# A decoder layer with grouped experts: residual added where the expert outputs are written, and a last stage without TensorE

## The chip, the cores and the metric

The kernel runs on one core of a Trainium2 chip. The metric is the device time of one execution in microseconds (us). Times are medians over runs; the profile is of one execution, whose own time is given beside its span, the time from its first to its last instruction.

## What is computed

One step of a hybrid decoder layer, for 1024 prompt tokens and 64 sample tokens of width 1024, all in float32. The parts that matter here are the last two lines of the layer:

```
h = layer_norm(ALPHA * x + mix, ln1_g, ln1_b)
y = layer_norm(ALPHA * h + hier_moe(h, ...), ln2_g, ln2_b)
```

`hier_moe` sends each token to 2 of 32 experts (a group of 8 is picked first, then two in it). An expert computes `silu(h @ w_gate) * (h @ w_up) * gate`, 256 wide, and multiplies that by `w_down` back to 1024. A token's result is the sum of its two experts' rows. `layer_norm` takes mean and variance over the 1024 columns, scales by `1/sqrt(var + 1e-5)`, then multiplies by gamma and adds beta.

## The kernel before

The kernel works in stages that follow each other behind barriers: input projection and convolutions; gated delta rule, output projection and the first layer norm in tiles of 128 tokens (writing `h_dram`); routing, which fills a table of slots per expert; the experts; and a last stage with the second layer norm.

**The expert stage** (lines 1578 to 1849) runs 24 passes (`NPASS`) and then one more per full block of 128 slots that does not fit, here a single one. A pass handles 128 slots, 96 of an expert of its own and 32 of one expert that three passes share. Its steps, with their engines:

- POOL gathers the pass's rows of h from `h_dram` into `xg` by an indirect DMA (`gather`, L1650). There are two buffers, and a gather waits until TensorE has turned the rows that the buffer held (`xg_turned`).
- TensorE transposes them (`turn_x`, L1694), ACT and DVE copy half each out of PSUM (L1768, L1816), TensorE multiplies by the gate and up weights (`gate_up`), ACT and DVE form the activation (L1773, L1821), TensorE transposes it (`turn_ac`, L1700) and multiplies by the down weights (`down`).
- ACT and DVE copy half of the result each from PSUM to `yo` (`out_s` L1782, `out_v` L1826), and POOL scatters it to `picked_dram` by an indirect DMA (`scatter`, L1656). That array has two rows per token, one for each of its picks.

TensorE's order in pass q is written out by hand: `turn_x(q+1)`, `gate_up(q)`, `down(q-1)`, `turn_ac(q)`. POOL's is `gather(q+3)`, then `scatter(q-1)`. The weights (2 MB and 1 MB per pass, and as much again for each third pass's shared expert) come on SP's DMA queue into three buffers (`NA`), each load waiting for the pass that used the buffer. After the last of them SP loads all of h, nine tiles of 512 KB, into `hres` (L1622) for the last stage.

**The last stage** (L1851 to L2012) takes nine tiles of 128 tokens. SP loads a tile's two picks (`picked`, 1 MB). TensorE adds them with four products by the identity and so into PSUM (L1942). DVE forms `ALPHA * hres + ysum` (L1984), two `bn_stats` (L1988), `bn_aggr`, and two tiny operations on mean and variance (L1992, L1993). POOL raises the variance to the power -0.5 (L1914) and forms the shift (L1917). ACT normalises (L1951), DVE multiplies by gamma (L2000), POOL adds beta (L1922), and ACT issues the store (L1956). Three buffers rotate, and each engine works one tile behind the one before it: `both` does the front of tile t and then the gamma or beta step of tile t-1.

## Time and profile before

| What | Value |
|---|---|
| Median of 3 runs | 1169.77 us (1169.17 to 1171.09) |
| The profiled execution's own time | 1168.77 us |
| Its span | 1167.0 us, mean granted TensorE clock 0.915 |
| Busy over the span | PE 83%, DVE 34%, ACT 15%, POOL 19% |
| Experts, from the first gather to the last scatter's issue | 768.3 to 1103.5 us |
| Last stage, from the first load | 1108.5 to 1167.0 us |

The span's last 400 us are the experts and the last stage. The shares are means over stages with different limits, so each stage is read by itself.

### The profile page before, as it was taken

To read this page: it belongs to the slowest core of one execution; us is meant where nothing else is said; L and a number is where in the kernel's file an instruction comes from. 1 tells how busy PE (TensorE), PEld (TensorE's weight loads), DVE (VectorE), ACT (ScalarE), POOL (GpSimd) and SP (SyncE) were. 2 spreads that over 40 slices of the span, in tenths; PEclk is the share of its full clock that TensorE was granted. 3 is DMA by queue.
4 is the path that set the end of the run, shared out by engine and by line. 5 is a ranking of instruction groups with operands and counts; after the bars stand their busy time and mean duration, and the time that the engine had idled before them with its cause. 6 is when DMAs were issued, how large, how long until landed. Compare 5 with 4: busy or idle time off the path is not lost. (4 is left out here: it accounts for less than half of the span.)

```text
span 1167.0 us, 13262 instructions
## 1 busy us (share of the span) xinstructions
PE 971.8 (83%) x5403; PEld 547.1 (47%) x5403; DVE 393.2 (34%) x737; ACT 173.5 (15%) x357; POOL 226.7 (19%) x238
## 2 busy tenths in 40 slices
PE   6999999999887999999988762049999999995583
PEld 4666666655445666666765422023333333331231
DVE  0434332586005554545542344201111111110056
ACT  1222233111021111111100000011111111110012
POOL 1011111220013222221113100611121211201047
PEclk9999999999888999999998875569999999998787
DMA  6011110202425011110031007757999999996094
GB/s 259 19 37 37 37 37 32 61 34 56 142 76 184 10 46 37 45 45 31 24 112 51 28 1 279 276 161 291 378 422 418 414 411 387 395 391 235 0 332 163
DMA packets 61323, 186.51 MB, mean 160 GB/s; under 512 B 22984, under 2 KB 36328, under 8 KB 51720
## 3 DMA queue, kind: packets, MB, share of 16 engines
q1 hardware_dynamic: 34640, 157.73, 35.3%
q0 software_dynamic: 8208, 19.09, 4.4%
q10 hardware_dynamic: 18416, 8.86, 2.7%
q8 instruction: 43, 0.70, 0.2%
q14 instruction: 16, 0.13, 0.0%
HBM read 164.15 MB, written 30.01 MB: 166 GB/s over the span
## 5 line engine op out<-in xcount | busy, mean ns | idle before, releaser
L359 PE MATMUL pj<-xT,wblk 128*128 128x384 f32 (+1 forms) x960 | 300.0, 474 | 18.3 <-DMA xT<-in_xt_dram 9.2
L359 PEld LDWEIGHTS pj<-xT,wblk 128*128 128x128 f32 x960 | 183.3, 192 | 129.8 <-issue 17.7
L1708 PE MATMUL e<-wgu_s,xgT 128*32 128x512 f32 x384 | 170.9, 598 | 0.0
L1708 PE MATMUL e<-wgu_a,xgT 128*32 128x512 f32 x768 | 114.7, 600 | 6.2 <-issue 3.2
L1708 PE MATMUL e<-wdn_a,acT 128*32 128x512 f32 x576 | 86.8, 592 | 0.7 <-ACT acT L1777 0.7
L1708 PE MATMUL e<-szT,acT 128*32 128x512 f32 x192 | 86.3, 592 | 0.0
L1694 PE MATMUL e<-cst,xg 128*128 128x128 f32 x200 | 28.7, 291 | 65.2 <-DMA xg<-h_dram,lst 48.4
L994 PE MATMUL b<-wout,yaT 128*128 128x512 f32 x144 | 69.7, 630 | 3.8 <-DVE yaT L1319 3.8
L1821 DVE SCALAR_TENSOR_TENSOR ac<-sg,lst,e 128x256 f32<-128x256 f32 x24 | 11.5, 480 | 171.2 <-ACT sg L1773 171.2
L1656 POOL DMA_INDIRECT picked_dram<-yo,lst x24 | 24.1, 1005 | 229.3 <-PE e L1694 185.0
L1708 PEld LDWEIGHTS e<-wgu_a,xgT 128*32 128x32 f32 x768 | 32.3, 111 | 75.9 <-issue 72.4
L994 PE MATMUL b<-wout,ybt 128*128 128x512 f32 x144 | 65.1, 595 | 0.0
L1708 PE MATMUL e<-qkvT,xgT 128*32 128x512 f32 x384 | 56.5, 594 | 0.0
L1694 PEld LDWEIGHTS e<-cst,xg 128*128 128x128 f32 x200 | 24.6, 151 | 67.3 <-DMA xg<-h_dram,lst 50.5
L1708 PEld LDWEIGHTS e<-wdn_a,acT 128*32 128x32 f32 x576 | 24.7, 110 | 56.7 <-issue 55.7
L626 DVE SCALAR_TENSOR_TENSOR cv<-raw,small,cv 128x1112 f32<-128x1112 f32 x36 | 49.6, 1377 | 1.3
L1942 PE MATMUL ysum<-picked,cst 128*128 128x512 f32 x72 | 33.9, 634 | 12.5 <-DMA picked<-picked_dram 12.5
L624 DVE TENSOR_SCALAR cv<-raw,small 128x1112 f32<-128x1112 f32 x12 | 9.6, 800 | 102.8 <-ACT raw L473 102.7
L994 PEld LDWEIGHTS b<-wout,yaT 128*128 128x128 f32 x144 | 27.7, 202 | 33.4 <-issue 28.8
L1708 PEld LDWEIGHTS e<-wgu_s,xgT 128*32 128x32 f32 x384 | 40.5, 110 | 0.0
L1826 DVE COPY yo<-e 128x512 f32<-128x512 f32 x25 | 17.3, 692 | 68.1 <-PE e L1708 63.3
L1816 DVE COPY xgT<-e 128x512 f32<-128x512 f32 x25 | 17.3, 691 | 66.0 <-PE e L1694 66.0
(321 smaller groups left out, 1248.4 us busy)
## 6 DMA issues: line engine op xcount, KB each, us to landing
wgu_a<-in_w_gate_up_dram SPq DMA_DIRECT2D x17, 2048.0 KB, 22.4
wdn_a<-in_w_down_dram SPq DMA_DIRECT2D x25, 1024.0 KB, 13.9
wgu_s<-in_w_gate_up_dram SPq DMA_DIRECT2D x8, 2048.0 KB, 15.6
qkvT<-in_w_gate_up_dram SPq DMA_DIRECT2D x8, 2048.0 KB, 19.4
wblk<-in_wcol_dram SPq DMA_DIRECT2D x20, 512.0 KB, 3.3
szT<-in_w_down_dram SPq DMA_DIRECT2D x8, 1024.0 KB, 18.1
picked<-picked_dram SPq DMA_DIRECT2D x8, 1024.0 KB, 5.7
h_dram<-h SPq DMA_DIRECT2D x9, 512.0 KB, 2.6
```

Of the source, the lines that this page charges most:

```text
L359: last = pe.matmul(pj[par][:, bank * 512:bank * 512 + m], wblk[par][:, k, :], xT[:, k, a:a + m], start=(k == 0), stop=(k == KT - 1))
L624: ins = dve.tensor_scalar(out, raw[par][:, 0:CFLAT], w, None, ALU.mult)
L626: ins = dve.scalar_tensor_tensor(out=out, in0=raw[par][:, j:CFLAT + j], scalar=w, in1=out, op0=ALU.mult, op1=ALU.add)
L994: last = pe.matmul(b[6 + half][:, :], src[:, kk, :], wout[:, k, half * 512:(half + 1) * 512], start=(k == H), stop=(k == H - 1))
L1656: pool.indirect_dma_start(y2_d, bass.IndirectOffsetOnAxis(ap=lst[:, q, 0:1], axis=0), yo[q % 2][:, :], None, bounds_check=2 * TP - 1, oob_ ...
L1694: last = pe.transpose(bank[:, at:at + P], xg[k][:, c * P:(c + 1) * P], C("ident"))
L1708: last = pe.matmul(out[at, :], lhsT[:, at], theirs if j == GROUP - 1 else mine, start=start, stop=stop)
L1816: dve.tensor_copy(xgT[k][:, H:, :].rearrange("p c t -> p (c t)"), b[1][:, :]).then_inc(xgT_ready, 1)
L1821: dve.scalar_tensor_tensor(out=ac[k][:, :], in0=sg[k][:, :], scalar=entry.bitcast(F32), in1=b[2 + k][:, FE:], op0=ALU.mult, op1=ALU.mult). ...
L1826: dve.tensor_copy(yo[k][:, 512:], b[7][:, :]).then_inc(yo_ready, 1)
L1942: last = pe.matmul(ysum[k][:, half * 512:(half + 1) * 512], C("ident"), picked[k][:, at:at + 512], start=(pick == 0), stop=(pick == 1))
```

## The change

- Each slot's table entry had the token number in its fourth word; it now has ALPHA for the first pick and 0 for the second.
- `out_v` does both halves on DVE: yo = (fourth word) x (gathered row) + (product in PSUM). ACT's `out_s` is gone. The sum of a token's two picks thus holds ALPHA * h.
- The gathered row must stay until then. `xg` has four buffers (`NX`), two of them in the space of `hres`, and `gather(q)` waits for `yo_ready` of pass q-4 where it waited for `xg_turned` of pass q-2. POOL issues four gathers first, and then in turn `scatter(q-1)`, `gather(q+3)`.
- The nine loads of `hres` are gone.
- The last stage has no TensorE work. DVE adds the two picks (`tensor_tensor`, both inputs in SBUF), takes the statistics, and after ACT's square root does a reciprocal and the shift. ACT normalises into a new tile `fin`. Gamma is split: DVE takes columns 0 to 511 (of the tile before), POOL columns 512 to 1023, then POOL adds beta to the whole. SP issues the stores, ACT the loads of gamma and beta. Four buffers rotate, and the loops are written out.

```
         rows_of = qkvT[:, :, :].rearrange("p c t -> p (c t)")
-        hres = rows_of[:, 0:NT * D].rearrange("p (t d) -> p t d", d=D)
...
                     for k in range(2):
-                        dve.tensor_copy(entry[:, k, :, 3], C("token"))
+                        dve.memset(entry[:, k, :, 3].bitcast(F32), ALPHA if k == 0 else 0.0)
                         dve.tensor_copy(entry[:, k, :, 1], C("token"))
...
-            xg, xgT = two("xg", [P, D]), two("xgT", [P, KT, P])
+            NX = 4
+            xg = [sb(f"xg{k}", [P, D], ctx=c4)[:, :] for k in range(2)] + [rows_of[:, k * D:(k + 1) * D] for k in range(2)]
+            xgT = two("xgT", [P, KT, P])
...
                         if q % (GROUP - 1) == GROUP - 2 and g < NE // GROUP:
                             load_shared_gu(g)
                             load_shared_dn(g)
-                    for t in range(NT):
-                        sp.dma_start(hres[:, t, :], h_d[t * P:(t + 1) * P, :]).then_inc(hres_in, 16)
-
...
-                    for k in pr:
-                        pool.memset(xg[k][:, :], 0.0).then_inc(cleared, 1)
-                    e.wait_ge(cleared, 2)
+                    for k in range(NX):
+                        pool.memset(xg[k], 0.0).then_inc(cleared, 1)
+                    e.wait_ge(cleared, NX)
...
                     def gather(q):
                         if q % (GROUP - 1) == 0:
                             e.wait_ge(lst_in[q // (GROUP - 1)], 32)
-                        wait(e, xg_turned, q - 1)
-                        pool.indirect_dma_start(xg[q % 2][:, :], None, h_d,
+                        wait(e, yo_ready, 2 * (q - NX + 1))
+                        pool.indirect_dma_start(xg[q % NX], None, h_d,
...
                     def scatter(q):
                         e.wait_ge(yo_ready, 2 * q + 2)
                         pool.indirect_dma_start(y2_d, bass.IndirectOffsetOnAxis(ap=lst[:, q, 0:1], axis=0),
                                                 yo[q % 2][:, :], None, bounds_check=2 * TP - 1, oob_is_err=False
                                                 ).then_inc(ov_scattered if q == last else scattered[q % 2], 16)
-                    for q in range(3):
+                    for q in range(NX):
                         gather(q)
-                    for q in range(NPASS):
-                        if q + 3 < NPASS:
-                            gather(q + 3)
-                        if q >= 1:
-                            scatter(q - 1)
+                    for q in range(1, NPASS):
+                        scatter(q - 1)
+                        if q + NX - 1 < NPASS:
+                            gather(q + NX - 1)
...
                     def turn_x(i, k):
                         wait(e, xgT_ready, 2 * i)
+                        rows = xg[k]
                         for c in range(KT):
                             bank, at = b[c // H], (c % H) * P
-                            last = pe.transpose(bank[:, at:at + P], xg[k][:, c * P:(c + 1) * P], C("ident"))
+                            last = pe.transpose(bank[:, at:at + P], rows[:, c * P:(c + 1) * P], C("ident"))
                         last.then_inc(xg_turned, 1)
...
                         if q + 1 < NPASS:
-                            e.wait_ge(gathered[(q + 1) % 2], 16 * ((q + 1) // 2) + 16)
-                            turn_x(q + 1, (q + 1) % 2)
+                            e.wait_ge(gathered[(q + 1) % NX], 16 * ((q + 1) // NX) + 16)
+                            turn_x(q + 1, (q + 1) % NX)
...
-                def out_s(e, i, k):
-                    e.wait_ge(dn_done, i + 1)
-                    act.activation(yo[k][:, 0:512], b[6][:, :], ACT.Copy).then_inc(yo_ready, 1)
...
                         silu(e, q, q % 2)
-                        if q >= 1:
-                            wait(e, scattered[(q - 1) % 2], 16 * ((q - 1) // 2))
-                            out_s(e, q - 1, (q - 1) % 2)
                         ac_turned_s(e, q, q % 2)
...
-                def out_v(e, i, k):
+                def out_v(e, i, k, rows, entry):
                     e.wait_ge(dn_done, i + 1)
-                    dve.tensor_copy(yo[k][:, 512:], b[7][:, :]).then_inc(yo_ready, 1)
+                    for half in range(2):
+                        c = slice(half * 512, (half + 1) * 512)
+                        dve.scalar_tensor_tensor(out=yo[k][:, c], in0=rows[:, c], scalar=entry.bitcast(F32),
+                                                 in1=b[6 + half][:, :], op0=ALU.mult, op1=ALU.add).then_inc(yo_ready, 1)
...
-            NB = 3
+            NB = 4
...
-            picked, res = each("picked", [P, 2 * D]), each("res", [P, D])
+            picked, res, fin = each("picked", [P, 2 * D]), each("res", [P, D]), each("fin", [P, D])
...
-            ysum = [pb(f"ysum{k}", [P, D], c5) for k in pr]
...
             with nc.Block() as block:
                 @block.sync
                 def _(e):
                     y2_v = y2_d.rearrange("(t k) d -> t (k d)", k=2)
...
+                    for t in range(NT):
+                        wait(e, summed, t - NB + 1)
+                        m = rows_in(t)
+                        sp.dma_start(picked[t % NB][0:m, :], y2_v[t * P:t * P + m, :]).then_inc(in_ready[t % NB], 16)
+                    for t in range(NT):
+                        m = rows_in(t)
+                        e.wait_ge(out_ready, t + 1)
+                        out = ys_o.rearrange("s t d -> (s t) d") if t == PT else yp_o[0, t * P:(t + 1) * P, :]
+                        sp.dma_start(out, fin[t % NB][0:m, :]).then_inc(stored[t % NB], 16)
...
+                @block.scalar
+                def _(e):
+                    act.dma_start(lng[:, :], ln2g_d.broadcast_to((P, D))).then_inc(ln_in, 16)
+                    act.dma_start(lnb[:, :], ln2b_d.broadcast_to((P, D))).then_inc(ln_in, 16)
+                    e.wait_ge(eps_ready, 1)
+                    for t in range(NT):
+                        k = t % NB
+                        e.wait_ge(var_ready, t + 1)
+                        act.activation(dev[k][:, :], mv[k][:, 1:2], ACT.Sqrt, bias=eps[:, :]).then_inc(dev_ready, 1)
+                        e.wait_ge(shift_ready, t + 1)
+                        wait(e, stored[k], 16 * (t // NB))
+                        act.activation(fin[k][:, :], res[k][:, :], ACT.Identity, scale=rstd[k][:, :],
+                                       bias=shift[k][:, :]).then_inc(normed, 1)
 
                 @block.gpsimd
                 def _(e):
+                    pool.memset(eps[:, :], LN_EPS).then_inc(eps_ready, 1)
                     e.wait_ge(ln_in, 32)
...
-                        pool.tensor_tensor(rstd[k][:, :], mv[k][:, 1:2], mhalf[:, 0:1], ALU.pow).then_inc(rstd1[k], 1)
...
-                        pool.tensor_tensor(shift[k][:, :], mv[k][:, 0:1], rstd[k][:, :], ALU.mult
-                                           ).then_inc(rstd_ready[k], 1)
...
-                        e.wait_ge(g_ready[k], i + 1)
-                        pool.tensor_tensor(done(i, k), done(i, k), lnb[:, :], ALU.add).then_inc(out_ready[k], 1)
...
+                    for t in range(NT):
+                        k = t % NB
+                        e.wait_ge(normed, t + 1)
+                        pool.tensor_tensor(fin[k][:, hi], fin[k][:, hi], lng[:, hi], ALU.mult).then_inc(scaled_p, 1)
+                        e.wait_ge(scaled_p, t + 1)
+                        e.wait_ge(scaled_v, t + 1)
+                        pool.tensor_tensor(fin[k][:, :], fin[k][:, :], lnb[:, :], ALU.add).then_inc(out_ready, 1)
 
                 @block.vector
                 def _(e):
...
-                        dve.scalar_tensor_tensor(out=r, in0=done(i, k), scalar=ALPHA, in1=ysum[k][:, :],
-                                                 op0=ALU.mult, op1=ALU.add).then_inc(ysum_read[k], 1)
...
+                    def front(t):
+
+                        k, m = t % NB, rows_in(t)
+                        e.wait_ge(in_ready[k], 16 * (t // NB) + 16)
+                        wait(e, normed, t - NB + 1)
+                        dve.tensor_tensor(res[k][0:m, :], picked[k][0:m, 0:D], picked[k][0:m, D:], ALU.add
+                                          ).then_inc(summed, 1)
+                        e.wait_ge(summed, t + 1)
+                        for half, c in enumerate((lo, hi)):
+                            last = dve.bn_stats(stats[k][:, half, :], res[k][:, c])
                         link(last)
...
-                        link(dve.bn_aggr(mv[k][:, :], stats[k][:, :, :].rearrange("p a b -> p (a b)")))
-                        dve.tensor_scalar(mv[k][:, 0:1], mv[k][:, 0:1], -1.0, None, ALU.mult)
-                        dve.tensor_scalar(mv[k][:, 1:2], mv[k][:, 1:2], LN_EPS, None, ALU.add
-                                          ).then_inc(var_ready[k], 1)
...
+                        dve.bn_aggr(mv[k][:, :], stats[k][:, :, :].rearrange("p a b -> p (a b)")).then_inc(var_ready, 1)
+
+                    def scale(t):
+
+                        k = t % NB
+                        if t == 0:
...
-                        dve.tensor_tensor(done(i, k), done(i, k), lng[:, :], ALU.mult).then_inc(g_ready[k], 1)
+                        e.wait_ge(normed, t + 1)
+                        dve.tensor_tensor(fin[k][:, lo], fin[k][:, lo], lng[:, lo], ALU.mult).then_inc(scaled_v, 1)
+
+                    def finish(t):
+
+                        k = t % NB
+                        e.wait_ge(dev_ready, t + 1)
+                        link(dve.reciprocal(rstd[k][:, :], dev[k][:, :]))
+                        dve.scalar_tensor_tensor(out=shift[k][:, :], in0=mv[k][:, 0:1], scalar=-1.0, in1=rstd[k][:, :],
+                                                 op0=ALU.mult, op1=ALU.mult).then_inc(shift_ready, 1)
+                    for t in range(NT):
+                        front(t)
+                        if t >= 1:
+                            scale(t - 1)
+                        finish(t)
+                    scale(NT - 1)
```

On POOL's queue, at the start of the expert stage, before (`picked_dram<-yo` is a scatter, `xg<-h_dram` a gather):

```order
L1639 MEMSET xg 128x1024 x2
L1650 DMA xg<-h_dram,lst 128x1024 x5
L1656 DMA picked_dram<-yo,lst 2304x1024
L1650 DMA xg<-h_dram,lst 128x1024
L1656 DMA picked_dram<-yo,lst 2304x1024
L1650 DMA xg<-h_dram,lst 128x1024
```

and now (the two buffers in the old `hres` space go by the name `qkvT`):

```order
L1636 MEMSET xg 128x1024 x2
L1636 MEMSET qkvT 128x1024 x2
L1647 DMA xg<-h_dram,lst 128x1024 x2
L1647 DMA qkvT<-h_dram,lst 128x1024 x2
L1653 DMA picked_dram<-yo,lst 2304x1024
L1647 DMA xg<-h_dram,lst 128x1024
L1653 DMA picked_dram<-yo,lst 2304x1024
```

Five gathers stood ahead of the first scatter, and now four: from there on a gather is issued behind the same scatter as before, but for the pass before the one it served.

On DVE's queue, one tile in the last stage's loop, before:

```order
L1984 SCALAR_TENSOR_TENSOR res<-qkvT,ysum 128x1024
L1988 BN_STATS stats<-res 128x6 x2
L1990 MEMSET spare 128x1
L1991 BN_AGGR mv<-stats 128x2
L1992 TENSOR_SCALAR mv<-mv 128x1
L1993 TENSOR_SCALAR mv<-mv 128x1
L2000 TENSOR_TENSOR qkvT<-qkvT,ln2g 128x1024
```

and now:

```order
L1922 TENSOR_TENSOR res<-picked 128x1024
L1926 BN_STATS stats<-res 128x6 x2
L1928 MEMSET spare 128x1
L1929 BN_AGGR mv<-stats 128x2
L1937 TENSOR_TENSOR fin<-fin,ln2g 128x512
L1943 RECIPROCAL rstd<-dev 128x1
L1944 SCALAR_TENSOR_TENSOR shift<-mv,rstd 128x1
```

The first operation now has both inputs in SBUF, the gamma step is half as wide, and the reciprocal and the shift stand behind it, before the next tile's sum.

## Rows read from the trace of the kernel before

**Rows 1.** Windows: us, PE, PEld, DVE, ACT, POOL busy, PE clock, DMA share, GB/s

```profile
845.00:892.00 47.00, 46.84 (x432) 16.99 (x424) 7.46 (x12) 7.41 (x16) 8.07 (x8) 1.00 1.01 421
```

**Rows 2.** Timeline, PE's idle gaps in passes: start, us, instruction, [idle before]

```profile
918.79 0.63 PE L1708 MATMUL e<-wgu_a,xgT 128*32 128x512 f32 x3 [1.67 <-DVE xgT L1816]
...
956.39 0.63 PE L1708 MATMUL e<-wgu_a,xgT 128*32 128x512 f32 x3 [2.49 <-issue]
...
992.89 0.63 PE L1708 MATMUL e<-wgu_a,xgT 128*32 128x512 f32 x3 [1.39 <-DVE xgT L1816]
```

**Rows 3.** Timeline, two pass boundaries: PE's transposes of gathered rows

```profile
799.05 1.04 PE L1694 MATMUL e<-cst,xg 128*128 128x128 f32 x8
...
810.73 1.04 PE L1694 MATMUL e<-cst,xg 128*128 128x128 f32 x8
```

**Rows 4.** Timeline, the first of these boundaries: DVE's copy, POOL's scatter and gather

```profile
798.91 0.69 DVE L1826 COPY yo<-e 128x512 f32<-128x512 f32 x1 [2.54 <-PE e L1708]
...
800.40 1.00 POOL L1656 DMA_INDIRECT picked_dram<-yo,lst  x1 [10.23 <-PE e L1694]
801.71 1.01 POOL L1650 DMA_INDIRECT xg<-h_dram,lst  x1 [0.30 <-issue]
```

**Rows 5.** DMA issues: gathers of 801.71, 825.14, all 19 after 801.6; median us to landing

```profile
xg<-h_dram,lst POOLq DMA_INDIRECT x1, 9.8
...
xg<-h_dram,lst POOLq DMA_INDIRECT x1, 14.3
...
xg<-h_dram,lst POOLq DMA_INDIRECT x19, 13.3
```

**Rows 6.** Groups by line and form, DVE: busy us, mean ns

```profile
L1210 DVE SCALAR_TENSOR_TENSOR xt<-xt,b 128x512 f32<-128x512 f32 x18 | 11.6, 683 | 28.0 <-PE b L994 28.0
```

**Rows 7.** Timeline, SP's queue: the loads of `hres`

```profile
1039.43 7.81 SPq L1622 DMA_DIRECT2D qkvT<-h_dram  x9
```

**Rows 8.** Timeline, last stage: the first loads and the last store

```profile
1108.47 0.81 SPq L1882 DMA_DIRECT2D picked<-picked_dram  x2
...
1162.41 0.61 ACTq L1967 DMA_DIRECT2D out_dram<-qkvT  x1
```

**Rows 9.** DMA issues of the first two loads there: count, KB each, median us to landing

```profile
picked<-picked_dram SPq DMA_DIRECT2D x2, 1024.0 KB, 6.0
```

**Rows 10.** Timeline, one tile of the last stage, DVE, POOL and ACT

```profile
1128.39 1.29 DVE L1988 BATCH_NORM_STATS2 stats<-res 128x6 f32<-128x512 f32 x2
1129.72 0.20 DVE L1991 BATCH_NORM_AGGREGATE mv<-stats 128x2 f32<-128x12 f32 x1
...
1130.09 1.22 DVE L2000 TENSOR_TENSOR qkvT<-qkvT,ln2g 128x1024 f32<-128x1024 f32 x1
...
1130.26 1.46 POOL L1914 TENSOR_TENSOR rstd<-mv,mhalf 128x1 f32<-128x1 f32 x1
...
1131.94 2.37 POOL L1922 TENSOR_TENSOR qkvT<-qkvT,ln2b 128x1024 f32<-128x1024 f32 x1
1132.02 1.24 ACT L1951 ACTIVATE qkvT<-res,shift,rstd 128x1024 f32<-128x1024 f32 x1 [2.84 <-POOL shift L1917]
```

**Rows 11.** Timeline, an earlier stage: DVE with two SBUF inputs beside POOL

```profile
352.60 2.37 POOL L959 TENSOR_TENSOR kq<-qkvT,egr 128x1024 f32<-128x1024 f32 x1
352.72 2.82 DVE L1332 TENSOR_TENSOR dT<-dT,rn2b 128x512 f32<-128x512 f32 x1 [0.85 <-POOL dT L955]
```

**Rows 12.** Groups by form: mean ns of such steps, the power in an earlier stage

```profile
L1332 DVE TENSOR_TENSOR dT<-dT,rn2b 128x512 f32<-128x512 f32 x7 | 4.8, 684 | 0.0
...
L946 POOL TENSOR_TENSOR rstd<-mv,mhalf 128x1 f32<-128x1 f32 x9 | 5.0, 550 | 167.1 <-DVE mv L1225 167.1
...
L955 POOL TENSOR_TENSOR dT<-dT,cst 128x512 f32<-128x512 f32 x9 | 11.4, 1271 | 8.1 <-ACT dT L1160 8.1
```

**Rows 13.** Groups: ACT's table load and a small ACT step

```profile
L1773 ACT ACT_TABLE_LOAD x1 | 1.3, 1283 | 0.0
L1464 ACT ACTIVATE gb<-ga 128x36 f32<-128x36 f32 x1 | 0.2, 232 | 10.3 <-DVE ga L1492 10.3
```

More of the change, by code:

```diff
@@ L1864, in build, with rows_in @@
             stats, mv = each("stats2", [P, 2, 6]), each("mv2", [P, 2])
[L1865 removed]
+            dev, rstd, shift = each("dev2", [P, 1]), each("rstd2", [P, 1]), each("shift2", [P, 1])
+            eps = sb("eps2", [P, 1], ctx=c5)
             spare = sb("spare5", [P, 1], ctx=c5)
[L1867 removed]
             S = phase(c5)
[L1869 to L1873 removed]
+            ln_in, chn, eps_ready = S("ln2_in"), S("chn2"), S("eps_ready")
+            in_ready, stored = ([S(f"{n}{k}") for k in pr] for n in ("in_ready", "stored"))
+            summed, var_ready, dev_ready, shift_ready, normed, scaled_v, scaled_p, out_ready = (S(n) for n in (
+                "summed", "var_ready", "dev_ready", "shift_ready", "normed", "scaled_v", "scaled_p", "out_ready"))
+            lo, hi = slice(0, D // 2), slice(D // 2, D)
+            def rows_in(t):
+                return NS if t == PT else P
             with nc.Block() as block:
@@ L1888, in _ @@
-                    load(0, 2)
-                    with e.Fori(1, NT // NB - 1) as i:
-                        for k in pr:
-                            load(i, k)
-                    for k in pr:
-                        load(NT // NB - 1, k, P if k < NB - 1 else NS)
-                    for k in pr:
-                        e.wait_ge(stored[k], 16 * (NT // NB))
-                def done(i, k):
-                    return hres[:, ds(NB * i + k, 1), :].rearrange("p a d -> p (a d)")
-                def rounds(e, step):
-                    def body(i):
-                        for k in pr:
-                            step(i, k)
-                    turns(e, NT // NB, body)
+                    for t in range(NT):
+                        wait(e, summed, t - NB + 1)
+                        m = rows_in(t)
+                        sp.dma_start(picked[t % NB][0:m, :], y2_v[t * P:t * P + m, :]).then_inc(in_ready[t % NB], 16)
@@ L1920, in add_bias @@
-                    def add_bias(i, k):
-                        e.wait_ge(g_ready[k], i + 1)
-                        pool.tensor_tensor(done(i, k), done(i, k), lnb[:, :], ALU.add).then_inc(out_ready[k], 1)
-                    def both(i, k):
-                        step(i, k)
-                        if k > 0:
-                            add_bias(i, k - 1)
-                        elif not isinstance(i, int):
-                            add_bias(i - 1, NB - 1)
-                    rounds(e, both)
@@ L1931, in _ @@
-                    add_bias(NT // NB - 1, NB - 1)
-                @block.tensor
-                def _(e):
-                    def step(i, k):
-                        e.wait_ge(in_ready[k], 16 * i + 16)
-                        wait(e, ysum_read[k], i)
-                        for half in range(2):
-                            for pick in range(2):
-                                at = pick * D + half * 512
-                                last = pe.matmul(ysum[k][:, half * 512:(half + 1) * 512], C("ident"),
-                                                 picked[k][:, at:at + 512], start=(pick == 0), stop=(pick == 1))
-                        last.then_inc(summed[k], 1)
-                    rounds(e, step)
@@ L1947, in _ @@
-                @block.scalar
-                def _(e):
-                    def step(i, k):
-                        e.wait_ge(rstd_ready[k], i + 1)
-                        act.activation(done(i, k), res[k][:, :], ACT.Identity, scale=rstd[k][:, :],
-                                       bias=shift[k][:, :]).then_inc(norm_ready[k], 1)
-                    def store(i, k):
-                        e.wait_ge(out_ready[k], i + 1)
-                        act.dma_start(yp_o[0, ds((NB * i + k) * P, P), :], done(i, k)).then_inc(stored[k], 16)
-                    def both(i, k):
-                        step(i, k)
-                        if k > 0:
-                            store(i, k - 1)
-                        elif not isinstance(i, int):
-                            store(i - 1, NB - 1)
-                    rounds(e, both)
-                    e.wait_ge(out_ready[NB - 1], NT // NB)
-                    act.dma_start(ys_o.rearrange("s t d -> (s t) d"), hres[0:NS, NT - 1, :]
-                                  ).then_inc(stored[NB - 1], 16)
+                    for t in range(NT):
[5 more added lines that the diff above has]
+                        pool.tensor_tensor(fin[k][:, :], fin[k][:, :], lnb[:, :], ALU.add).then_inc(out_ready, 1)
@@ L1970, in _ @@
                 @block.vector
                 def _(e):
-                    def front(i, k):
-                        at = (NB * i + k) * 2
-                        ln = [0]
-                        def link(ins):
-                            ln[0] += 1
-                            ins.then_inc(chn, 1)
-                            e.wait_ge(chn, at + ln[0])
-                        e.wait_ge(summed[k], i + 1)
-                        wait(e, norm_ready[k], i)
-                        r = res[k][:, :]
-                        dve.scalar_tensor_tensor(out=r, in0=done(i, k), scalar=ALPHA, in1=ysum[k][:, :],
-                                                 op0=ALU.mult, op1=ALU.add).then_inc(ysum_read[k], 1)
-                        e.wait_ge(ysum_read[k], i + 1)
-                        for half in range(2):
-                            last = dve.bn_stats(stats[k][:, half, :], r[:, half * 512:(half + 1) * 512])
+                    chain = [0]
```

52 lines of the change are left out of this document (12 added, 40 removed).

## The prediction

> **What bounds the kernel now.** I read the windows first, to see which resource is full in the expert stage, then the waits of TensorE there, then the timeline of one pass boundary and of one tile in the last stage. Over 47 us in the middle of the expert stage TensorE is busy for 46.84 us at the full clock (1.00, its 2.4 GHz level), and at the same time the DMA engines' share is 1.01 [rows 1]. Two limits lie on top of each other: a pass is 11.68 us of TensorE work (799.05 to 810.73 [rows 3]), and its transfers take about as long. TensorE's only sizeable gaps are three, of 1.67, 2.49 and 1.39 us, each before a `gate_up` [rows 2], whose inputs are the expert weights: 5.5 us in all. So the stage has no slack for a transfer that arrives later. In the last stage POOL is the bound: power, shift and beta follow each other without a gap from 1130.26 to 1134.31 [rows 10], about 4.1 us a tile, and the power takes 1.46 us there against 0.55 elsewhere [rows 10, 12].
>
> **The expert stage: the gather is issued later.** Before, the gather behind `scatter(0)` was the sixth, number 5, needed by `turn_x(5)` at the start of pass 4. Now it is number 4, needed at the start of pass 3. In the time of before: DVE's copy starts at 798.91 and takes 0.69, the scatter follows at 800.40 and the gather at 801.71 [rows 4]. Now DVE does both halves as multiply-adds from PSUM, and such steps take 0.683 us [rows 6], starting about 0.61 apart, so `yo` is ready 0.6 later and the gather starts at 802.3. The transposes that need it start at 810.73 [rows 3]: it has 8.4 us. Number 5 had 20.7 us before, from 801.71 to 810.73 + 11.68. Landings took 9.8 us at 801.71, 14.3 at 825.14, and 13.3 in the median of the 19 from 801.6 on [rows 5]. It is late.
>
> What a late gather costs is less than its lateness, for a stall S in one pass lengthens that pass and gives the next gather more time: S(n+1) = L - 8.4 - S(n), with L the landing time. So the mean stall is (L - 8.4)/2. Twenty gathers (4 to 23) are issued this way. L is unknown, for the stalls also thin the traffic. The bounds are from the rows: at 9.8 (the lightest such row) 0.7 us each, 14 us in all; at 13.3 (the full queue) 2.45 each, 49 us. A cycle of three passes has one with the shared expert's 3 MB on top. The rows nearest to a queue that starts nearly empty are 9.8, 9.8 and 14.3, mean 11.3; I take the middle between that and 13.3, L = 12.3, as the stalls let the queue drain only in part: 20 x 3.9/2 = 39 us. The 5.5 us of waits for weights [rows 2] are then gone, since TensorE asks for weights later. **Net +33.5 us**, ends +8.5 and +43.5.
>
> The rule of the Trainium skill on queues (DMA: Bandwidth & Descriptors, Queues, rings and completion order) says that a DMA engine takes turns between queue rows, a packet from each; read as equal halves, that would let a gather land before its deadline even beside the weights. The trace does not bear that reading out, with 13.3 us for half a megabyte at most; the case of a gather in time is the second rival.
>
> Other edits there. ACT's copies go, and DVE's second one is on no path in the passes: `down(q)` needs the bank only after a `gate_up`. In the single extra pass, and in the scatter that it waits for, it is: 0.6 us twice, **+1.2 us**. The loads of `hres` cost nothing now (issued from 1039.43 for 7.81 us [rows 7], when the last weights were requested, and awaited by nobody before the last stage), so their removal gives nothing. Two more clears of `xg` on POOL stand ahead of the first gather, where POOL has to wait for the lists of slots anyway.
>
> **The last stage.** From the first load's issue to the last store's it takes 1162.41 - 1108.47 = 53.94 us [rows 8]. What decides it now is whether DVE and POOL can read SBUF at the same time. They can't, if DVE has two inputs there [rows 11]: L1332 usually takes 0.684 us [rows 12] and took 2.82 beside a POOL operation that ended at 354.97, that is, it ran after it. In the other direction POOL's one-element power takes 1.46 instead of 0.55 us when DVE's gamma product (two inputs in SBUF) began just before [rows 10, 12]. Before, only that product was of this kind. Now the sum, the gamma half and the shift are, beside POOL's gamma half and beta.
>
> One period, from the end of a DVE gamma half: POOL starts beta after 0.06 and holds the port for 2.35; DVE's reciprocal (0.2, as the aggregate) fits beside it, its shift must wait and ends at 2.6; the next sum takes 1.2 (as L2000 [rows 10]), to 3.8; the statistics 1.29, to 5.1, while ACT normalises and POOL does its gamma half (1.27, L955 [rows 12]); the aggregate with its links 0.26; DVE's gamma half 0.68: **6.0 us** per tile against 4.1. Whether a one-element DVE step waits too no row shows; if not, the period is 5.84 (the sum then waits), and the stage 2.7 us less. I take 6.0, after POOL's one-element step.
>
> The Trainium skill (SBUF — State Buffer, Who interferes with whom) calls the port pair an exclusive lock and names DVE steps with two SBUF inputs beside a POOL read, of any size. By it the shift waits as well, and the period would be 6.0.
>
> The sum in steps: first load 6.0 [rows 9], with gamma and beta now beside it; sum, statistics and aggregate 2.75; table load 1.28 and square root 0.23 [rows 13]; reciprocal, shift and links 0.5; seven periods 42.1 (tile 1 to tile 8); sum, statistics, aggregate of tile 8 2.75; then gamma half of tile 7 0.7, beta of tile 7 2.4, shift 0.2, normalise 1.3, DVE's half 0.7, POOL's half 1.3, beta 2.35: 9.0. Together 64.6 us, **+10.7**. The table load is on the path once (it stands behind the wait for the first variance). The same skill (ScalarE: Activation LUTs, What ACT_TABLE_LOAD costs) adds 1.38 us of drain to it, which no row here shows; the sum would be 12.1. TensorE's 72 products go, and save only the head, some 5 us, which is in this sum. SP's stores stand behind its last load; buffer 0 is stored just in time for tile 4.
>
> **Sum.** 33.5 + 1.2 + 10.7 = +45.4 us on the profiled execution, 1168.77 + 45.4 = 1214.2. The median lies 1.0 above that execution, so 1215.
>
> **Rivals.**
> - *The gathers are late, but the port is shared without exclusion* (10%). Against it stand [rows 11]. Then POOL is the bound with 1.27 + 2.35 us a tile, 3.7 with links, and the last stage takes 47.6 us, -6.3: 1169.8 + 33.5 + 1.2 - 6.3 = 1198.
> - *The gathers land in time* (6%). For it: a gather alone on thin traffic is small, and 9.8 is close to 8.4. Against it: no row after 801.6 is below 9.8. The stage then gains or loses nothing, or gains up to 5.5 if the weights also come earlier: 1169.8 + 1.2 + 10.7 = 1182, down to 1176.
> - *It gets faster, by the last stage* (3%): no exclusion, so the head that TensorE took is a gain and the stage is 6.3 us shorter. It decides the sign only where the expert stage costs less than 5 us net, 10 x (L - 8.4) - 5.5, that is for L below 9.4. With L = 8.4: 1169.8 + 1.2 - 6.3 = 1165.
> - *The change does less than it says*: if something else had long set the pass (weights), the later gather would hide behind it (1%, 1180). TensorE's 46.84 us in 47 [rows 1] speak against it.
> - The likeliest case has 80%.
>
> **How the numbers follow.** 1215 is the likeliest. Its own ends are 1169.8 + 8.5 + 1.2 + 8.0 = 1187 and 1169.8 + 43.5 + 1.2 + 13 = 1228, the 13 with a first load that is slowed by gamma and beta. The range of 8 in 10 takes in most of this and the first rival, 1186 to 1229. Runs of this kernel differ by 0.16%, so 0.2% is what a measurement can tell from no change. Faster takes the third rival, 0.03; same 0.02, where ends of the second and the third meet; slower 0.95.
>
> **What would show it.** In the changed profile: TensorE idle before the transposes of `xg`, released by the gathers, 1 to 6 us in most passes and some 35 to 40 in all, while the DMA share falls under 1.00; gaps before `gate_up` gone. In the last stage a period of 6.0 us, the shift on DVE lasting some 2 us though it has one element, and POOL waiting in turn. Wrong would be: gathers that land in under 8.4 us; a period of 3.7 to 4.1; or a granted clock under 1.00 in the passes, which the gaps could bring (it is 1.00 now [rows 1]) and which is not in the sum.

## The result, and the profile after

| | before | after |
|---|---|---|
| Median of 4 runs each | 1169.47 us (1166.23 to 1171.09) | 1219.95 us (1218.48 to 1222.14) |
| Ratio | | 1.0446, interval 1.0416 to 1.0475 |
| Profiled execution: own time, span, granted clock | 1168.77, 1167.0, 0.915 | 1218.81, 1217.0, 0.887 |

The kernel is 4.5% slower; the forecast was 1215 us. The profiled execution's span grew by 50.0 us. Cut at the same events in both traces:

| Stretch | Forecast | Measured |
|---|---|---|
| to the first `turn_x` (772.6, now 773.33) | 0 | +0.7 |
| first to last `turn_x` (266.6, now 308.24): waits for gathers | +39 | +32.3 |
| the same: waits for weights gone | -5.5 | -5.5 |
| the same: the rest, nearly all TensorE at its lower clock | not in the sum | +14.8 |
| last `turn_x` to the last stage's first load (69.25, now 70.1) | +1.2 | +0.9 |
| first load to last store (53.94, now 61.0) | +10.7 | +7.1 |
| behind the last store | 0 | -0.3 |

What TensorE waited for from 800 to 1085 us, in the profile's waits after (us in total, times, longest):

```profile
PE e L1691 <- DMA xg<-h_dram,lst: 18.1, 7, 5.8
PE e L1691 <- DMA qkvT<-h_dram,lst: 14.2, 7, 5.4
```

Both are `turn_x` waiting for its gathered rows (`qkvT` names the two buffers in the old space of `hres`). No wait for weights is left, where there were three [rows 2]. The boundary of pass 0 on POOL, in the timeline after (start, duration):

```profile
801.50 0.99 POOL L1653 DMA_INDIRECT picked_dram<-yo,lst  x1 [27.41 <-DVE yo L1813]
802.80 1.02 POOL L1647 DMA_INDIRECT xg<-h_dram,lst  x1 [0.30 <-issue]
813.18 1.00 POOL L1653 DMA_INDIRECT picked_dram<-yo,lst  x1 [9.37 <-DVE yo L1813]
814.48 1.00 POOL L1647 DMA_INDIRECT xg<-h_dram,lst  x1 [0.30 <-issue]
```

The first late gather starts at 802.80; 802.3 was forecast from [rows 4]. The 20 gathers from there on take 8.8 to 14.3 us to land, mean 11.66. TensorE behind some of its waits, in the timeline after:

```profile
811.75 1.09 PE L1691 MATMUL e<-cst,xg 128*128 128x128 f32 x8 [0.47 <-DMA xg<-h_dram,lst]
...
841.23 1.97 PE L1691 MATMUL e<-cst,qkvT 128*128 128x128 f32 x8 [5.41 <-DMA qkvT<-h_dram,lst]
843.13 1.08 PE L1705 MATMUL e<-qkvT,xgT 128*32 128x512 f32 x3
843.15 1.06 PE L1705 MATMUL e<-wgu_s,xgT 128*32 128x512 f32 x1
...
868.72 1.41 PE L1691 MATMUL e<-cst,xg 128*128 128x128 f32 x8 [1.90 <-DMA xg<-h_dram,lst]
...
884.09 1.10 PE L1691 MATMUL e<-cst,xg 128*128 128x128 f32 x8 [1.84 <-DMA xg<-h_dram,lst]
...
969.00 1.97 PE L1691 MATMUL e<-cst,qkvT 128*128 128x128 f32 x8 [4.15 <-DMA qkvT<-h_dram,lst]
```

Behind waits of 0.47 and 1.84 us the eight transposes take 1.1 us. Behind those of 4 us and more they take 1.97, and the first products then 1.08, where they take 0.6 otherwise. Behind the wait of 1.90 us the transposes are slowed half-way (1.41). The windows after show the reason in their granted clock (columns: window, its length, busy us and count of PE, PEld, DVE, ACT and POOL, granted clock, DMA share, GB/s); the last row is the window of [rows 1]:

```profile
834.80:838.00 3.20, 1.03 (x10) 0.20 (x2) 1.41 (x2) 0.38 (x1) 0.20 (x1) 1.00 1.04 434
838.00:841.20 3.20, 0.00 (x0) 0.00 (x0) 0.00 (x0) 0.00 (x0) 1.81 (x2) 0.60 1.02 435
841.20:843.00 1.80, 1.77 (x8) 1.57 (x8) 0.00 (x0) 0.00 (x0) 0.00 (x0) 0.50 0.96 394
843.00:845.00 2.00, 2.00 (x13) 0.56 (x16) 0.69 (x1) 0.60 (x1) 0.00 (x0) 0.50 1.02 428
845.00:847.00 2.00, 2.00 (x24) 0.53 (x20) 0.00 (x0) 0.00 (x0) 0.00 (x0) 0.89 1.08 455
...
845.00:892.00 47.00, 43.26 (x378) 14.00 (x374) 7.64 (x12) 4.10 (x9) 6.05 (x6) 0.96 0.90 361
```

The clock falls to 0.50 (1.2 GHz) while TensorE is idle, stays there for some 4 us of work, and is back at 1.00 (2.4 GHz) by 847. So this pass takes 13.74 us from 841.23, and not 11.68 [rows 3]. Six passes are long in this way: those from 841.23, 868.72, 926.34, 969.00, 998.03 and 1054.41, by 2.1, 1.9, 2.2, 3.0, 1.9 and 3.0 us without the waits at their ends, some 14 of the 14.8. In the two long by 3.0 us the clock stays low for 6 us of work. Four of them follow waits of 4.15 to 5.79 us, two (868.72, 998.03) waits of 1.90 and 2.48.

The last stage, one tile on DVE and POOL, in the timeline after:

```profile
1171.39 0.64 DVE L1937 TENSOR_TENSOR fin<-fin,ln2g 128x512 f32<-128x512 f32 x1
1171.94 0.15 DVE L1943 RECIPROCAL rstd<-dev 128x1 f32<-128x1 f32 x1
1172.13 0.16 DVE L1944 SCALAR_TENSOR_TENSOR shift<-mv,rstd 128x1 f32<-128x1 f32 x1
1172.21 3.39 DVE L1922 TENSOR_TENSOR res<-picked 128x1024 f32<-128x1024 f32 x1
1175.63 1.29 DVE L1926 BATCH_NORM_STATS2 stats<-res 128x6 f32<-128x512 f32 x2
1176.96 0.20 DVE L1929 BATCH_NORM_AGGREGATE mv<-stats 128x2 f32<-128x12 f32 x1
1177.08 0.64 DVE L1937 TENSOR_TENSOR fin<-fin,ln2g 128x512 f32<-128x512 f32 x1
```

```profile
1172.17 2.34 POOL L1906 TENSOR_TENSOR fin<-fin,ln2b 128x1024 f32<-128x1024 f32 x1 [1.14 <-DVE fin L1937]
1174.48 2.24 POOL L1903 TENSOR_TENSOR fin<-fin,ln2g 128x512 f32<-128x512 f32 x1
```

DVE's sum, 1.2 us of work (each is 1.22 in e7 below), is recorded with 3.39 us: POOL's beta started 0.04 us before it, ends at 1174.51, and the sum ends 1.1 us later. It waited for beta; e6 and e7 below test this. POOL's gamma half then waits for the sum (2.24 us where alone it takes 1.26). The period (from one tile to the next) is 5.70 us, against 4.1 before [rows 10]. It changes once, at ACT's fifth normalisation (ACT, SP and DVE after):

```profile
1188.04 1.24 ACT L1893 ACTIVATE fin<-res,shift,rstd 128x1024 f32<-128x1024 f32 x1 [4.85 <-DMA out_dram<-fin]
```

```profile
1151.70 30.10 SPq L1873 DMA_DIRECT2D picked<-picked_dram  x9
1181.84 31.40 SPq L1878 DMA_DIRECT2D out_dram<-fin  x9
```

```profile
1190.11 1.03 DVE L1944 SCALAR_TENSOR_TENSOR shift<-mv,rstd 128x1 f32<-128x1 f32 x1
1191.06 1.21 DVE L1922 TENSOR_TENSOR res<-picked 128x1024 f32<-128x1024 f32 x1
```

Buffer 0 isn't stored in time, since SP issues its first store at 1181.84, behind all nine loads. After that wait the two engines meet in another order: now the one-element shift is the step that waits, the sum takes 1.21 us, POOL's beta waits for it (3.28), and the period is 5.02 us.

### The profile page after: what moved, and what is told of

The parts are those of the page before. It is cut to its first block and busy times, and to the rows that moved or that the text cites. A ratio compares the mean times of both kernels' runs of the same rounds, so it can differ in the third digit from the quotient of the medians.

```text
span 1217.0 us, 13017 instructions
## 1 busy us (share of the span) xinstructions
PE 952.6 (78%) x5331; PEld 532.5 (44%) x5331; DVE 419.7 (34%) x762; ACT 165.1 (14%) x342; POOL 234.1 (19%) x232
## 5 line engine op out<-in xcount | busy, mean ns | idle before, releaser
L1705 PE MATMUL e<-wgu_s,xgT 128*32 128x512 f32 x384 | 180.0, 624 | 0.0
L1705 PE MATMUL e<-wgu_a,xgT 128*32 128x512 f32 x768 | 117.3, 612 | 0.0
L1691 PE MATMUL e<-cst,xg 128*128 128x128 f32 x104 | 18.7, 339 | 85.0 <-DMA xg<-h_dram,lst 67.2
L1705 PE MATMUL e<-qkvT,xgT 128*32 128x512 f32 x384 | 63.1, 649 | 0.0
L1691 PEld LDWEIGHTS e<-cst,xg 128*128 128x128 f32 x104 | 15.0, 174 | 88.8 <-DMA xg<-h_dram,lst 69.7
L994 PEld LDWEIGHTS b<-wout,ybt 128*128 128x128 f32 x144 | 26.0, 190 | 26.2 <-issue 26.2
L946 POOL TENSOR_TENSOR rstd<-mv,mhalf 128x1 f32<-128x1 f32 x9 | 5.0, 552 | 167.0 <-DVE mv L1225 167.0
```

Source lines behind the costliest of these rows:

```text
L994: last = pe.matmul(b[6 + half][:, :], src[:, kk, :], wout[:, k, half * 512:(half + 1) * 512], start=(k == H), stop=(k == H - 1))
L1691: last = pe.transpose(bank[:, at:at + P], rows[:, c * P:(c + 1) * P], C("ident"))
L1705: last = pe.matmul(out[at, :], lhsT[:, at], theirs if j == GROUP - 1 else mine, start=start, stop=stop)
```

## The experiments

**e1: a fifth row buffer.** If the late gathers are what the expert stage lost by, letting each start one pass earlier must give it all back, clock included.

```
-            NX = 4
+            NX = 5
...
-            xg = [...] + [rows_of[:, k * D:(k + 1) * D] for k in range(2)]
+            xg = [...] + [rows_of[:, k * D:(k + 1) * D] for k in range(3)]
```

> The changed kernel with five buffers for gathered rows (NX = 5), so that a gather is again issued two passes ahead. Theory (late gathers): the 32 us of waits for gathers and the 14 us that the passes lose at the lower clock both go, the waits for weights (5.5 us) come back; what is left against the kernel before is the last stage (+7), the extra pass (+1) and the clears (+1): 1178 to 1180 us. Rival (the lateness is not the cause; DVE's doubled copy or the holding of rows until the outputs are written is): still above 1210 us.

1180.22 us (1177.97 to 1181.22), at the upper end of the forecast; ratio to before 1.0083 [1.0057, 1.0108]. (The ratios of the experiments are to runs of the kernel before that were made beside them, medians 1169.66 us for e1 to e4 and 1170.18 for e5 to e8.) TensorE's waits in e1 from 798 us on and a window of the passes (columns as above):

```profile
PE e L1705 <- issue: 3.4, 1, 3.4
PE e L1705 <- DVE xgT L1801: 1.5, 1, 1.5
PE e L1705 <- DVE yo L1813: 1.3, 1, 1.3
...
PE e L1705 <- ACT xgT L1765: 0.9, 1, 0.9
```

```profile
845.00:892.00 47.00, 47.00 (x432) 16.43 (x428) 9.95 (x16) 5.46 (x12) 8.06 (x8) 1.00 1.01 421
```

No gather is waited for in the passes, the waits before `gate_up` are back, and in this window clock and DMA share stand at 1.00 and 1.01 as in [rows 1]. (Behind the one wait of 3.4 us the clock was at 0.50 for some 2.6 us of work.) From first to last `turn_x` it takes 267.1 us (before 266.6). So the whole of the +41.6 us came from when the gathers start; the multiply-adds on DVE and the residual in the table cost the passes 0.5 us at most. Of the 11.6 us by which e1's profiled span is still above that of before, 6.8 are the last stage and 3.6 stand ahead of the first `turn_x`. Of these, 3.2 are there already when POOL starts its first clear, ahead of anything that the edit touches.

**e2: the kernel before, with the gathers late.** Only POOL's order is changed, to that of the change; two buffers, `hres` and the old last stage stay.

```
-                    for q in range(3):
+                    for q in range(4):
                         gather(q)
-                    for q in range(NPASS):
+                    for q in range(1, NPASS):
+                        scatter(q - 1)
                         if q + 3 < NPASS:
                             gather(q + 3)
-                        if q >= 1:
-                            scatter(q - 1)
```

> The kernel before with POOL's order alone changed to that of the changed kernel (four gathers, then scatter(q-1) ahead of gather(q+3)); residual, loads of h and last stage as before. Theory (late gathers): the gather has 9.0 us (801.71 to 810.73), so waits of (11.7 - 9.0)/2 in 20 passes are 27 us, and falls of the clock add up to 14, less the 5.5 for weights: 1195 to 1206 us. Rival (the residual in the expert stage or the missing loads of h cost the time): 1169 to 1172 us.

1206.46 us (1200.06 to 1210.76), half a microsecond over the forecast; ratio 1.0293 [1.0256, 1.0330]. Its runs spread over 10.7 us, those of e1 over 3.3, so its middle is less sure. Its waits and one window:

```profile
PE e L1693 <- DMA xg<-h_dram,lst: 29.5, 14, 5.0
```

```profile
900.00:947.00 47.00, 42.00 (x360) 14.07 (x362) 6.29 (x10) 6.16 (x13) 6.05 (x6) 0.91 0.80 319
```

Fourteen waits as in the change, and a fallen clock. In the profiled execution, the slowest of the four, first to last `turn_x` is 306.2 us, +39.6: of it 29.5 waits, -5.5 weights, and again a rest of 15.6. The order alone makes the loss; what the change does on DVE and ACT isn't needed for it.

**e3: the change, with TensorE kept busy in the gaps.** Is the rest of 14.8 us the clock? Six products that nobody reads (into bank 0, once its last contents are copied) stand ahead of the waits for four of the gathers that came late.

```
+                        if q + 1 in (6, 12, 15, 21):
+                            wait(e, xgT_ready, 2 * (q + 1))
+                            for _ in range(6):
+                                pe.matmul(b[0][:, :], C("ident"), cst[:, 0:512], start=True, stop=True)
                         if q + 1 < NPASS:
                             e.wait_ge(gathered[(q + 1) % NX], 16 * ((q + 1) // NX) + 16)
```

> The changed kernel with six 128x512 products without use put on TensorE in front of the waits for gathers 6, 12, 15 and 21, the four behind which it waited over 4 us and the granted clock then fell; they write a PSUM bank that the transposes overwrite. Theory (the fallen clock lengthens those passes by 2.1, 2.2, 3.0 and 3.0 us): the clock stays at 1.00 in these stretches and the time falls by 5 to 10 us, to 1210 to 1215 us, though TensorE has more to do. Rival (these passes are long because of their transfers, the clock is a by-product): 1219 to 1222 us or more.

1214.39 us (1211.76 to 1215.73), ratio 1.0383 [1.0359, 1.0407], 5.6 us under the change though TensorE has more to do. What stands in its timeline where the change had the gap before 841.23 (the profile lists the six products as 12 records), and two windows where the change had such gaps:

```profile
836.73 5.32 PE L1737 MATMUL e<-cst 128*128 128x512 f32 x12
842.41 1.09 PE L1691 MATMUL e<-cst,qkvT 128*128 128x128 f32 x8 [0.37 <-DMA qkvT<-h_dram,lst]
```

```profile
834.00:852.00 18.00, 17.63 (x126) 6.37 (x122) 2.63 (x5) 1.36 (x3) 2.01 (x2) 1.00 1.01 426
918.00:936.00 18.00, 18.00 (x134) 6.54 (x130) 2.77 (x5) 1.36 (x3) 2.02 (x2) 1.00 1.00 419
```

The transposes start even later than in the change (842.41 for 841.23), and take 1.09 us and not 1.97. First to last `turn_x` is 299.6 us. Waits of 13.2 and four times 5.32 us of empty products make 34.5 us, 2.2 more than the change's 32.3 of waiting; with -5.5 for the weights a rest of 4 is left of the 14.8. So the lower clock in these four places made some 10 us of the rest. Net it cost less, 8.6 us from first to last `turn_x`, as the waits grew by those 2.2: a pass that isn't slowed leaves the next gather less time. The 4 that are left hold two new falls of the clock, behind waits of 3.21 and 4.38 us.

**e5 to e7: what sets the last stage.** All three start from e1. e5 issues the stores among the loads; e6 gives DVE the whole of gamma, so that POOL has only beta; e7 leaves POOL's work out, so the second half of its columns lacks gamma and all of them lack beta.

```
 e5 (SP), behind the load of tile t:
+                        if t >= NB + 1:
+                            store(t - NB - 1)
 e6 (POOL, DVE):
-                        pool.tensor_tensor(fin[k][:, hi], fin[k][:, hi], lng[:, hi], ALU.mult).then_inc(scaled_p, 1)
-                        e.wait_ge(scaled_p, t + 1)
...
-                        dve.tensor_tensor(fin[k][:, lo], fin[k][:, lo], lng[:, lo], ALU.mult).then_inc(scaled_v, 1)
+                        dve.tensor_tensor(fin[k][:, :], fin[k][:, :], lng[:, :], ALU.mult).then_inc(scaled_v, 1)
 e7 (POOL), in place of the gamma half and beta:
+                        pool.memset(eps2[:, t:t + 1], 0.0).then_inc(out_ready, 1)
```

> The kernel of the first experiment (the change with five row buffers, 1180.2 us) with one edit in the last stage: SP issues the store of tile t-5 behind the load of tile t, so that no store stands behind all nine loads. It removes one wait of ScalarE's final activation for a store, 4.5 us there. Theory of the port (vectorE and GpSimd hold each other off the tiles in SBUF, and the tile pace of 5.70 us comes from that): the wait was mostly slack, and the pace of 5.70 us now runs on to the end where it was 5.0 us after the wait, so the two about cancel: 1178 to 1182 us. Rival, the wait counted whole: 1175.7 us.

> The five-buffer kernel (1180.2 us) with gamma multiplied by vectorE on all 1024 columns (1.24 us in place of 0.64) and no gamma half on GpSimd, whose only work per tile is then the bias, 2.34 us. Where the two engines exclude each other, the tiles' period is gamma 1.2 + bias 2.3 + sum 1.2 + statistics 1.3 + 0.2 and about 0.2 of gaps, since the bias starts when gamma ends and holds the next sum off: 6.0 to 6.4 us, so 1182 to 1187 us, although GpSimd has less to do. Rival, no exclusion (the long sums of 3.4 us have another cause, such as the loads): vectorE's own work, 4.5 us a tile, sets the pace: about 1170 us.

> The five-buffer kernel (1180.2 us) with GpSimd's gamma half and bias left out of the last stage (the second half of the columns isn't scaled and no column gets its bias; one element is set instead, so that the order of the work stays). Exclusion: no sum takes 3.4 us any more, every one takes 1.2, the tile pace is vectorE's own 3.8 to 3.9 us instead of 5.7 to 5.0, and the end of the last tile is some 5 us shorter too: 1160 to 1166 us. Rival, the sums are slow because of the loads that land beside them: they keep 3.4 us, the pace stays at 5.7, and only the last tile's 4.6 us go: 1175.6 us.

| | Median, us | Ratio to before | Period in the trace |
|---|---|---|---|
| e1 | 1180.22 | 1.0083 [1.0057, 1.0108] | 5.70, then 5.0 |
| e5 | 1180.26 (1175.41 to 1182.22) | 1.0083 [1.0054, 1.0113] | 5.69 to the end |
| e6 | 1181.73 (1177.33 to 1184.06) | 1.0099 [1.0071, 1.0126] | 6.23 |
| e7 | 1163.46 (1158.61 to 1166.99) | 0.9948 [0.9929, 0.9967] | 3.53, but for one wait for a store |

Two tiles' sums on DVE in each, first e5, then e6 with its gamma and POOL's beta, then e7:

```profile
1134.02 3.38 DVE L1927 TENSOR_TENSOR res<-picked 128x1024 f32<-128x1024 f32 x1
...
1139.72 3.38 DVE L1927 TENSOR_TENSOR res<-picked 128x1024 f32<-128x1024 f32 x1
```

```profile
1139.19 1.17 DVE L1935 TENSOR_TENSOR fin<-fin,ln2g 128x1024 f32<-128x1024 f32 x1
...
1140.50 2.35 POOL L1904 TENSOR_TENSOR fin<-fin,ln2b 128x1024 f32<-128x1024 f32 x1 [3.88 <-DVE fin L1935]
...
1140.55 3.39 DVE L1920 TENSOR_TENSOR res<-picked 128x1024 f32<-128x1024 f32 x1
```

```profile
1126.78 1.22 DVE L1921 TENSOR_TENSOR res<-picked 128x1024 f32<-128x1024 f32 x1
...
1130.30 1.22 DVE L1921 TENSOR_TENSOR res<-picked 128x1024 f32<-128x1024 f32 x1
```

e6 is the sharpest: POOL has a third less to do and is idle for 3.88 us a tile, and still the period grows to 6.23 us, inside the 6.0 to 6.4 worked out for two engines that hold each other off. The rival, DVE's own work setting the pace, put the period at 4.5 us and the time at 1170 (e7's 3.53 and the wider gamma would make an estimated 4.1). The median is 0.3 us under the forecast and its interval overlaps e1's, so that e6 is slower than e1 rests on the period. e7 shows the other side: without POOL's operations no sum is long, at the same loads, and the period is DVE's own. The clash with POOL costs 2.2 us a tile at the pace of 5.70, and 1.5 at that of 5.02. e5 removes the wait for the store and gains nothing, because the pace of 5.69 us then goes on to the end: the wait was paid for by the better order behind it.

**e4, e8: a last stage without the clash.** The gathers early as in e1; TensorE sums the picks into PSUM as in the kernel before (without the multiply-add of `hres`, which the sum now holds); DVE reads PSUM for the statistics and for (sum - mean) x gamma; ACT scales by 1/deviation; POOL adds beta alone. e8 also issues the stores as e5 does.

```
+                                last = pe.matmul(ysum[k][:, half * 512:(half + 1) * 512], C("ident"),
+                                                 picked[k][:, at:at + 512], start=(pick == 0), stop=(pick == 1))
...
+                            last = dve.bn_stats(stats[k][:, half, :], ysum[k][:, c])
...
+                        dve.scalar_tensor_tensor(out=res[k][:, :], in0=ysum[k][:, :], scalar=mv[k][:, 0:1],
+                                                 in1=lng[:, :], op0=ALU.subtract, op1=ALU.mult).then_inc(scaled_v, 1)
...
+                        act.activation(fin[k][:, :], res[k][:, :], ACT.Copy, scale=rstd[k][:, :]).then_inc(normed, 1)
```

> Five buffers, and another last stage: TensorE adds the picks into PSUM as in the kernel before, the statistics read PSUM, DVE forms (sum - mean) * gamma in one step from PSUM and SBUF, ACT multiplies by 1/deviation, POOL adds beta alone. No DVE step has two inputs in SBUF, so by the theory of the exclusive port nothing holds POOL or DVE: the period is TensorE's 3.8 us, the stage some 50 us instead of 61, and the time 1166 to 1169 us. Rival (DVE and POOL slow each other whatever their inputs are): beta takes over 2.4 us or the DVE step over 1.3 us, and the time is 1172 us or more.

> The fourth experiment's kernel (1164.5 us) with the stores issued among the loads as in the fifth. ScalarE's wait of 6.5 us for a store goes. Its trace has a pace of 3.43 us a tile before the wait and 2.83 after it, and the last activation started at 1155.6 us; at 3.43 all the way it would start at 1126.9 + 8 x 3.43 = 1154.3. So 1162.5 to 1164.5 us, 1.3 below. Rival, the wait counted whole: 1158 us.

e4: 1164.52 us (1161.41 to 1167.44), ratio 0.9960 [0.9939, 0.9980]. e8: 1165.15 us (1160.91 to 1167.41), ratio 0.9961 [0.9943, 0.9978]. Both are better than the change, and 0.4% better than the kernel before, with intervals that leave out 1. DVE in e8:

```profile
1134.09 1.28 DVE L1948 SCALAR_TENSOR_TENSOR res<-ysum,mv,ln2g 128x1024 f32<-128x1024 f32 x1
1135.29 0.15 DVE L1951 RECIPROCAL rstd<-dev 128x1 f32<-128x1 f32 x1
1135.95 1.30 DVE L1937 BATCH_NORM_STATS2 stats<-ysum 128x6 f32<-128x512 f32 x2 [0.50 <-PE ysum L1897]
```

and POOL in e8:

```profile
1133.28 2.35 POOL L1922 TENSOR_TENSOR fin<-fin,ln2b 128x1024 f32<-128x1024 f32 x1 [0.53 <-ACT fin L1913]
```

The two run side by side at their own durations, the multiply at 1.28 us with one input in PSUM. DVE waits 0.50 us a tile for TensorE's sum, which makes the period of 3.43 us. With the other edits of this last stage made at the same time, the runs don't say what each is worth by itself; e4's forecast, 1166 to 1169 us, was too high, in part because it took 3.8 us for TensorE's period.

e4 has a wait of 6.5 us for the store and catches most of it up afterwards. The last activation on ACT, in e4 and in e8:

```profile
1155.60 1.15 ACT L1908 ACTIVATE fin<-res,rstd 128x1024 f32<-128x1024 f32 x1 [1.09 <-DVE rstd L1946]
```

```profile
1156.51 1.15 ACT L1913 ACTIVATE fin<-res,rstd 128x1024 f32<-128x1024 f32 x1 [1.09 <-DVE rstd L1951]
```

The last stage's first load stands at 1110.19 in e4 and at 1112.41 in e8. From there to this activation it is 45.4 us in e4 and 44.1 in e8: the forecast gain of 1.3 us is there in the traces. The medians don't show it (e8's lies 0.6 above e4's, within both spreads, and over the forecast), as the stages ahead of the last differ by more than that from run to run.

## Where the prediction held, and where not

- *The late gathers are the main loss*: held, and shown by e1 and e2. The first late gather had from 802.80 to 811.28, where `turn_x` began to wait: 8.5 us for the forecast 8.4. The formula 20 x (L - 8.4)/2 gives 32.6 us with the measured L of 11.66, against 32.3 of waits. That they agree so closely is partly luck: six of the 20 gathers had landed in time, where the formula lets a stall go under nought, and a pass at the lower clock hid part of the next wait, which it leaves out. The choice "L = 12.3" was too high: the nearest rows' mean, 11.3, would have been better than the middle between that and the full queue. In the four windows of 47 us from 845 to 1033 the DMA share was 0.81 to 0.94, before 0.96 to 1.01.
- *The clock*: this is the step that failed. "a granted clock under 1.00 in the passes, which the gaps could bring [...] and which is not in the sum" is a term put at nothing. It cost 14.8 us, near a third of the whole loss, and e3 took some 10 of them away. The mean stall of 1.6 us hides that the stalls come unevenly, four of them 4 to 6 us long, and the long ones bring the clock down: in the change nothing happened behind 0.28 to 1.84 us, and behind 1.90 us and more it fell each time. The forecast's total came near by luck: the waits were taken 7 us too high, the last stage 4 too high and the clock 15 too low.
- *DVE and POOL can't both read SBUF when DVE has two inputs there*: held (e6, e7). The Trainium skill (SBUF — State Buffer, Who interferes with whom) has their shared pair of ports as an exclusive lock, and the trace agrees: the shift's 1.03 us for 0.16 of work shows that a one-element step with two SBUF inputs waits as well. But the forecast had the shift wait in each tile, "6.0 us". It starts 0.04 us before beta (1172.13 and 1172.17) and slips through, and the sum waits in its place: 5.70, near the 5.84 given for that case. ("The stage 2.7 us less" doesn't follow from that: seven periods of 5.84 for 6.0 are 1.1 us less.)
- *The last stage, "+10.7"*: measured +7.1. From tile 1 to tile 8, by DVE's aggregate, four of the seven periods were 5.70, one 5.30 and the last two 5.02, in place of 6.0 each: 38.1 us for 42.1. "Buffer 0 is stored just in time for tile 4" was wrong by 4.85 us, which e5 shows to have cost nothing net. The first load landed in 6.5 us, 0.5 over the forecast; the table load took 1.28, as forecast. "TensorE's 72 products" are 36 (four a tile), which the profile lists as 72 records; no term hangs on it.
- *The drain of 1.38 us behind a table load* (the Trainium skill, ScalarE: Activation LUTs, What ACT_TABLE_LOAD costs): the table load is recorded from 1161.08 to 1162.36, and the square root starts at 1162.38 and takes 0.29 us. The trace doesn't agree: no drain is to be seen behind the load, and the +10.7 was right to leave it out.
- *DVE's second copy is on no path in the passes*: held for the passes (e1). For the last one it wasn't: there `down(23)` follows `down(22)` with no `gate_up` between, and TensorE waits 1.3 us for `yo` (the row "DVE yo L1813" of e1). With the extra pass the stretch still grew by only 0.9.
- *The rivals*: gathers in time, and reading SBUF without exclusion, are both ruled out by the rows above, and with them the two that rested on these or on slack in the passes. (The rival for "faster" leaves the 5.5 us of weights out of its 1165; with them it would be 1159.)

## What to carry to other kernels

When a buffer is to live longer (here so that a residual can be taken from it), count from the trace when its refill can start and when it is wanted, and add a buffer if the landing time is longer: one more here took back 40 us. Cost a stall on TensorE with its distribution and not its mean, for the long ones cost 2 to 3 us each on top at the lower clock. Before moving element work from PSUM into SBUF beside a busy GpSimd, look at which pairs of operations have both inputs in SBUF; with one input left in PSUM neither engine was held here, though TensorE then had to work for it.

## What the runs showed of the hardware that was not expected

- Waits of 4.15 to 5.79 us on TensorE dropped its granted clock to 0.50 before it worked again, and the work behind stayed at that level for 4 to 6 us: 2.1 to 3.0 us a time. Behind waits of 1.90 and 2.48 us the clock fell too, but only after work had begun again (1.9 us each); behind one of 1.84 it didn't. The length of a wait alone doesn't settle it: in e2 the clock was at 0.50 from 871 to 874 behind a wait of 1.83 us, in e3 it stayed at 1.00 behind one of 1.86, and before at 1.00 behind one of 2.49 ([rows 2], at 956.39). What does settle it these runs don't show.
- Which of DVE and POOL waits is settled by who starts first, and a lead of 0.04 us is enough. The same code ran at 5.70 us a tile, and, after a single disturbance, at 5.02. A wait removed (e5) or work moved off one engine (e6: a longer period with less for POOL to do) may therefore gain nothing.
- Gathers of up to 0.5 MB landed in 8.8 to 14.3 us beside the weights' queue although the DMA share was 0.81 to 0.94 in windows of 47 us: the mean share doesn't tell when a transfer lands.
